# Head pairs of the stick-breaking group in a written-out order, and sums of weight halves by accumulating transfers

## What is computed

```python
def stick_breaking(q, k, v):             # 8 heads of 128
    ...
        z = jnp.einsum('bthd,bshd->bhts', qb, k).astype(jnp.float32) * d_h ** -0.5
        mask = key_pos[None, :] < t_pos[:, None]
        lo = jnp.where(mask, jax.nn.log_sigmoid(-z), 0.0)
        rc = lax.cumsum(lo, axis=3, reverse=True)
        log_a = jax.nn.log_sigmoid(z) + (rc - lo)
        a = jnp.where(mask, jnp.exp(log_a), 0.0)
        return jnp.einsum('bhts,bshd->bthd', a.astype(v.dtype), v)

def squared_relu_mlp(n, w_up, w_down):   # 1024 -> 4096 -> 1024, once in each layer
    return jnp.square(jax.nn.relu(n @ w_up)) @ w_down
```

## Time and profile before

| | us |
|---|---|
| median of 3 runs | 1587.18 |
| lowest, highest | 1586.47, 1589.25 |
| the profiled execution's own time | 1587.28 |
| its span in the trace | 1585.4 |
| TensorE busy | 1562.2 |
| VectorE, ScalarE, GpSimd busy | 1036.8, 726.8, 678.2 |

### The profile page before, as it was taken

How to read it: one execution, slowest core, us unless ns; L and a number is a source line. 1 busy time by engine, 2 the same in 40 slices (tenths; PEclk the granted TensorE clock), 3 DMA queues, 4 the chain that set the end, 5 groups by cost and what they waited for, 6 DMA issues and landing times.

```text
span 1585.4 us, 20551 instructions
## 1 busy us (share of the span) xinstructions
PE 1562.2 (99%) x7570; PEld 1283.4 (81%) x7570; DVE 1036.8 (65%) x1343; ACT 726.8 (46%) x1085; POOL 678.2 (43%) x666
## 2 busy tenths in 40 slices
PE   9999999999999999999999999989999999999999
PEld 7888787787778898888888888768886888888887
DVE  7424554675678977458584848867777557584847
ACT  6323433324245655434353435566775443444434
POOL 0002120104346443285666667422333474757574
PEclk9999999999999999999999999989999999999999
DMA  7232222232211221323223231222120414141321
GB/s 245 80 106 80 79 79 79 95 106 84 103 53 54 93 66 66 135 80 117 97 106 106 87 126 40 70 77 71 63 80 27 160 54 159 54 145 68 134 80 54
DMA packets 25731, 145.07 MB, mean 92 GB/s; under 512 B 3936, under 2 KB 5680, under 8 KB 9264
## 3 DMA queue, kind: packets, MB, share of 16 engines
q1 hardware_dynamic: 25648, 143.95, 26.4%
HBM read 141.84 MB, written 2.10 MB: 91 GB/s over the span
## 4 chain that ended last, share of the span: by engine, by line
PE 88%; DVE 9%; ACT 2%; issue 1%; POOL 0%; DVEq 0%; ACTq 0%; POOLq 0%
PE ps_G L613 20%; PE ps_G L615 20%; PE ps_G L614 20%; PE ps_C L1245 5%; PE ps_C L1244 5%; PE ps_C L1243 5%; PE ps_C L699 1%; PE ps_AV L1076 1%; PE ps_AV L1244 1%; PE ps_AV L1243 1%; PE ps_AV L1245 1%; DVE wide L2619 1%; DVE top L2615 1%; PE ps_C L713 1%; DVE wide L2809 1%
## 5 line engine op out<-in xcount | busy, mean ns | idle before, releaser
L613 PE MATMUL ps_G<-ch,wh 128*128 128x512 f32 x800 | 320.0, 400 | 0.7 <-DVE cl L2279 0.5
L615 PE MATMUL ps_G<-ch,wl 128*128 128x512 f32 x800 | 312.3, 390 | 0.0
L614 PE MATMUL ps_G<-cl,wh 128*128 128x512 f32 x800 | 312.2, 390 | 0.0
L2925 DVE TENSOR_TENSOR wl<-raw,wh 128x1024 fp32r<-128x1024 f32 (+1 forms) x104 | 180.7, 1756 | 30.5 <-ACT wh L1878 25.1
L613 PE MATMUL ps_G<-nh,wh 128*128 128x512 f32 x504 | 199.7, 396 | 0.4 <-DVE h L2487 0.2
L615 PE MATMUL ps_G<-nh,wl 128*128 128x512 f32 x504 | 196.3, 390 | 0.0
L614 PE MATMUL ps_G<-nl,wh 128*128 128x512 f32 x504 | 196.2, 389 | 0.0
L613 PEld LDWEIGHTS ps_G<-ch,wh 128*128 128x128 f32 x800 | 150.8, 188 | 39.9 <-issue 7.6
L614 PEld LDWEIGHTS ps_G<-cl,wh 128*128 128x128 f32 x800 | 150.7, 188 | 33.8 <-issue 3.4
L615 PEld LDWEIGHTS ps_G<-ch,wl 128*128 128x128 f32 x800 | 150.6, 188 | 31.7
L2214 DVE TENSOR_TENSOR wl<-raw,wh 128x2048 fp32r<-128x2048 f32 x46 | 108.6, 2360 | 62.1 <-ACT wh L1385 58.9
(11 more groups left out here) (429 smaller groups left out, 3185.6 us busy)
## 6 DMA issues: line engine op xcount, KB each, us to landing
raw<-wst SPq DMA_DIRECT2D x96, 1024.0 KB, 4.9
raw<-quart_d SPq DMA_DIRECT2D x16, 1024.0 KB, 4.9
tabs<-quart_d SPq DMA_DIRECT2D x8, 1024.0 KB, 7.1
mixed_buffers<-quart_d SPq DMA_DIRECT2D x8, 1024.0 KB, 5.3
raw<-wst SPq DMA_DIRECT2D x8, 256.0 KB, 6.9
out<-wide SPq DMA_DIRECT2D x8, 256.0 KB, 2.0
h<-xT SPq DMA_DIRECT2D x7, 256.0 KB, 6.9
raw<-wst SPq DMA_DIRECT2D x2, 512.0 KB, 5.9
```

What stands on the lines that cost most here:

```text
L613: mm(o, ah, bh, start=first, stop=False)
L614: mm(o, ah, bl, start=False, stop=False)
L615: return mm(o, al, bh, start=False, stop=last)
L2925: return tt(lo, x, hi.bitcast(F), ALU.subtract)
```

## The change

**Stick-breaking.** In group 0, the split of weight tile 1 moves up on both engines: on ScalarE ahead of the second `evac_qk`, on VectorE ahead of `diagonals_of` (a product with the identity, from which the row scales of the values come). The weights of head 12, the first of the group, are formed in group 0 instead of group 1: on ScalarE the softplus is the last step there, and the last root (`rsqrt(("qk", qk0 + 3))`) goes to group 1; on VectorE the first half stands ahead of `apply(3)` and the second inside it. In group 1 ScalarE does the first `evac_qk`, the root, the exponential and then the split (before: split, softplus, evacuation, exponential), and TensorE turns the scores ahead of the statistic of block 0. Groups 2 and 3 keep their order.

**Feed-forward.** The sums of weights are made by transfers that add to their destination (`accum_op=ALU.add`), issued on GpSimd's queue. They can't subtract, so the scheme is taken with the opposite sign of the right column: T3 = B22 + B12, T1 = B12 + B11, T2 = B11 + B12 + B22, T4 = B21 + T2. GpSimd's value sums and the second pair change sign to match, and the accumulators of the right column subtract. SyncE loads B22 a second time, into `t3` (`load_third`). T2 takes two transfers, from DRAM, the second of which waits for the first (`t2_part`); T4's source is on the chip. Each sum has a semaphore of its own, for the whole sum rather than for each half.

**End of the first feed-forward half.** VectorE's `low(4, 2)` stands ahead of `final_add(3)`.

```diff
+            def load_third(pt):
+                sp.dma_start(t3, quart_d[pt.f, pt.p, B22]).then_inc(t3_load, 16)
...
                 load_quarter(pt, B12, b12)
+                load_third(pt)
                 load_quarter(pt, B22, b22)
...
-                    sp.wait_ge(weight_sums, pt.sums_w + 8)
+                    sp.wait_ge(t4_in, 16 * (pt.g + 1))
                     sp.wait_ge(half_lo, pt.half(2, 1))
                     load(t % 2, t)
                     if not pt.last:
+                        sp.wait_ge(half_lo, pt.half(3, 1))
+                        load_third(Part(f, p + 1))
                         sp.wait_ge(half_lo, pt.half(4, 1))
                         load_quarter(Part(f, p + 1), B12, b12)
...
                 if name == "stick" and g == 1:
                     head_stat(("qk", qk0 - 1))
-                block_(1, 0, P)
-                head_stat(("qk", qk0))
-                if prev is not None:
+                    block_(1, 0, P)
+                    do_turns(0)
+                    head_stat(("qk", qk0))
+                else:
+                    block_(1, 0, P)
+                    head_stat(("qk", qk0))
                     do_turns(0)
...
                     evac_qk(0, 0)
+                    split(st, 1)
                     evac_qk(1, 1)
-                    split(st, 1)
...
+                    values_out(wide[:, 13, :], st, 5, 1)
                     rsqrt(("qk", qk0 + 2))
-                    values_out(wide[:, 13, :], st, 5, 1)
-                    rsqrt(("qk", qk0 + 3))
+                    weights(hd)
                     return
-                split(st, 0)
-                if prev is not None:
+                if g == 1:
+                    evac_qk(0, 0)
+                    rsqrt(("qk", qk0 - 1))
+                    exponential(prev)
+                    split(st, 0)
+                else:
+                    split(st, 0)
                     weights(prev)
-                evac_qk(0, 0)
-                if prev is not None:
+                    evac_qk(0, 0)
                     exponential(prev)
...
-                            act.wait_ge(weight_sums, pt.sums_w + W_SUMMED[i] + a + 1)
+                            act.wait_ge(W_SUMMED[i], 16 * (pt.g + 1))
...
-                    def weight_sum(dst, x, y):
...
+                    def add_weights(dst, x, sem_):
+
+                        g.dma_start(dst, quart_d[f, p, x] if isinstance(x, int) else x, accum_op=ALU.add).then_inc(sem_, 16)
...
+                    pool.wait_ge(t3_load, 16 * (pt.g + 1))
+                    add_weights(t3, B12, t3_in)
                     pool.wait_ge(quarter_in[B12], 16 * (pt.g + 1))
-                    pool.wait_ge(quarter_in[B22], 16 * (pt.g + 1))
+                    add_weights(b12, B11, t1_in)
                     if pt.g:
                         pool.wait_ge(half_lo, pt.halves)
-                    weight_sum(t3, b22, b12)
                     pair_sums(0)
                     pair_sums(1)
-                    pool.wait_ge(quarter_in[B11], 16 * (pt.g + 1))
-                    weight_sum(b12, b12, b11)
                     pair_sums(2)
                     pool.wait_ge(half_lo, pt.half(0, 1))
-                    pool.wait_ge(weight_sums, pt.sums_w + 4)
-                    weight_sum(b11, b22, b12)
+                    add_weights(b11, B12, t2_part)
+                    pool.wait_ge(t2_part, 16 * (pt.g + 1))
+                    add_weights(b11, B22, t2_in)
                     pair_sums(3)
                     pool.wait_ge(half_lo, pt.half(1, 1))
-                    pool.wait_ge(weight_sums, pt.sums_w + 6)
-                    weight_sum(b21, b21, b11)
+                    pool.wait_ge(t2_in, 16 * (pt.g + 1))
+                    add_weights(b21, b11, t4_in)
...
+                    split(st, 1)
                     diagonals_of(tmp[:, 5, :])
-                    split(st, 1)
                     apply(0, lambda: token_scales(2))
                     apply(1)
                     split(st, 2)
                     apply(2)
-                    apply(3)
+                    weights(hd, part=0)
+                    apply(3, lambda: weights(hd, part=1))
                     return
-                if prev is not None:
+                if prev is not None and (soft or g > 1):
                     weights(prev)
...
                 low(4, 1)
-                add_up(6, X, 0, 1)
+                add_up(6, X, 0, 1, ALU.subtract)
+                low(4, 2)
                 final_add(3)
-                low(4, 2)
```

More of the change, by code:

```diff
@@ L84, in __init__ @@
         self.first, self.last = p == 0, p == 3
-        self.halves, self.sums_w, self.sums_a = 14 * self.g, 8 * self.g, 16 * self.g
+        self.halves, self.sums_a = 14 * self.g, 16 * self.g
         self.adds = (4 * ADDS + 2) * f + ADDS * p
@@ L242, in build @@
         hid_set, quarter_in = sem("hid_set"), [sem(f"quarter_in{q}") for q in range(4)]
-        weight_sums, value_sums = sem("weight_sums"), sem("value_sums")
+        t1_in, t2_part, t2_in, t3_load, t3_in, t4_in = (sem(n) for n in (
+            "t1_in", "t2_part", "t2_in", "t3_load", "t3_in", "t4_in"))
+        value_sums = sem("value_sums")
         half_hi, half_lo, half_done = sem("half_hi"), sem("half_lo"), sem("half_done")
@@ L442, in build @@
         RING = (0, 1, 2, 3, 0, 2, 1)
-        W_SUMMED = {3: 0, 4: 2, 2: 4, 5: 6}
+        W_SUMMED = {2: t2_in, 3: t3_in, 4: t1_in, 5: t4_in}
         BACK = ("C2", "AV", "SX", "ST", "C2", "AV", "SX", "ST")
@@ L1895, in second_pair @@
                         act.wait_ge(value_sums, pt.sums_a + 4 * c + 3)
-                        A(ring_hi[:, 2:4, c, :], wide[:, 2 * c, :].rearrange("p (s n) -> p s n", s=2), ACT.Copy).then_inc(
+                        A(ring_hi[:, 2:4, c, :], wide[:, 2 * c, :].rearrange("p (s n) -> p s n", s=2), ACT.Copy, scale=-1.0).then_inc(
                             second_pair_hi, 1)
@@ L2113, in layer @@
                     b11, b21 = part_weights(pt)[0:2]
-                    def weight_sum(dst, x, y):
-                        for a in range(2):
-                            for n in range(4 * a, 4 * a + 4):
-                                w = slice(n * TW, (n + 1) * TW)
-                                ins = g.tensor_tensor(dst[:, w], x[:, w], y[:, w], ALU.subtract)
-                            ins.then_inc(weight_sums, 1)
+                    def add_weights(dst, x, sem_):
+                        g.dma_start(dst, quart_d[f, p, x] if isinstance(x, int) else x, accum_op=ALU.add).then_inc(sem_, 16)
                     def value_sum(n, dst, x, y, op):
@@ L2132, in pair_sums @@
                         pool.wait_ge(hid_set, 8 * pt.g + 2 * c + 2)
-                        value_sum(n, s1[:, c, :], a21, a22, ALU.add)
-                        value_sum(n + 1, a21, a11, a21, ALU.subtract)
+                        value_sum(n, s1[:, c, :], a22, a21, ALU.subtract)
+                        value_sum(n + 1, a21, a21, a11, ALU.subtract)
                         pool.wait_ge(first_pair_lo, 4 * pt.g + c + 1)
                         pool.wait_ge(value_sums, n + 2)
-                        value_sum(n + 2, a11, s1[:, c, :], a11, ALU.subtract)
+                        value_sum(n + 2, a11, a11, s1[:, c, :], ALU.add)
                         pool.wait_ge(value_sums, n + 3)
-                        value_sum(n + 3, a12, a12, a11, ALU.subtract)
+                        value_sum(n + 3, a12, a11, a12, ALU.subtract)
                     if pt.first and not f:
@@ L2781, in rotated, with weights @@
                     dve.wait_ge(q_rot, n + 1)
-                def weights(hh, whole=True, last=None):
+                def weights(hh, whole=True, last=None, part=None):
                     Sb = MIX_Sb[side(hh)]
@@ L2801, in weights @@
                     for n, banks in enumerate(HALVES):
+                        if part not in (None, n):
+                            continue
                         dve.wait_ge(sp_log, 2 * (hh - 12) + n + 1)
@@ L2935, in second_pair, with add_up @@
                         dve.wait_ge(second_pair_hi, 4 * pt.g + c + 1)
-                        subtract(ring_hi[:, 2:4, c, :], ring_lo[:, 2:4, c, :],
-                                 wide[:, 2 * c, :].rearrange("p (s n) -> p s n", s=2)).then_inc(second_pair_lo, 1)
-                    def add_up(i, banks, t, n):
+                        stt(out=ring_lo[:, 2:4, c, :], in0=wide[:, 2 * c, :].rearrange("p (s n) -> p s n", s=2),
+                            scalar=-1.0, in1=ring_hi[:, 2:4, c, :].bitcast(F), op0=ALU.mult,
+                            op1=ALU.subtract).then_inc(second_pair_lo, 1)
+                    def add_up(i, banks, t, n, op=ALU.add):
                         dve.wait_ge(half_done, pt.half(i, 1))
@@ L2944, in add_up @@
                             to = accumulator(2 * t + b, n)
-                            tt(to, to, ps[banks[b]][:], ALU.add).then_inc(acc_added, 1)
+                            tt(to, to, ps[banks[b]][:], op).then_inc(acc_added, 1)
```

(6 more changed lines are left out.)

## The result

The changed kernel took **1630.8 us** (median of 4 runs, 1628.3 to 1633.5) beside 1587.0 us for the kernel before (1586.5 to 1589.3): ratio 1.0276, 95% interval 1.026 to 1.0293. It is 44 us slower. The forecast was 1578.8 us, with a range of 1571 to 1612; the sign was wrong and the time lies outside the range.

The account below looks back on a forecast made before the run. TensorE, busy 99% of the span, was taken as the bound, leaving only idle time and slow clock to win. Span 1585.4 - 8 (opening) - 0.4 (low(4, 2)) = 1577.0, transfers 0, giving 1578.8 us measured; range 1571 to 1612.

Parts of the forecast that it names:

- the middle: Feed-forward weight sums: 6.1 us for each accumulating 1 MB transfer, so T2 is in at 804.7 and nothing is late.
- The upper end: Feed-forward weight sums: an accumulating megabyte also reads its destination, 7.4 us, making T2 2.1 us late in each part.
- the lower end: Feed-forward weight sums: an accumulating megabyte takes 4.9 us, as a plain load of the same array does; nothing late.
- The price of the clock behind a pause: Feed-forward, behind each pause before product 2: 1.2 us of slow clock, from 1.7 us behind the old 2.54 us pause.
- Rival A: Feed-forward: T2's chain of two transfers ends late, eight pauses; 1606 us at 7.4 us per transfer; chance 0.36.
- The opening: Start of stick-breaking: the new order gains 8 us, from 5 to 11.
- near tie: Opening, head pair 0: TensorE reaches the scores at 1039.5 with inputs ready at 1039.1; 2 to 3 us counted.
- Rival B: Opening of stick-breaking: new waits replace old ones, so 3 us gained instead of 8, 1584 us; chance 0.07.
- low(4, 2) ahead of an addition: End of the first feed-forward half: moving the correction ahead gains 0.4 us, from 0 to 0.5.
- GpSimd's sums removed for 0 us: Feed-forward: taking 257 us of weight sums off GpSimd is by itself worth nothing, as TensorE never waited for them.
- T1, T3, T4 and the signs: Feed-forward: T3 and T1 have over 40 us of cover, T4 is wanted after 16 us, moved signs cost 0 us.
- Rival C: Feed-forward: accumulating transfers delay the load of the next part's second tile, 1 us a part, 1587 us; chance 0.04.

Follow-up runs that it names:

- e1: Kernel before with only the new order of the head pairs and low(4, 2), weight sums still on GpSimd: 1579.7 us, ratio 0.9964.
- e9: Second run of the kernel before with the new order alone, weight sums on GpSimd: 1579.8 us, ratio 0.9951.
- e3: Changed kernel with T2 made by one accumulating transfer, B11 += T3: 1576.4 us, ratio 0.994 to the kernel before.
- e10: Second run of the changed kernel with T2 made by one transfer from T3: 1577.5 us, ratio 0.9935 to the kernel before.
- e8: Kernel before with old order, weight sums by four accumulating transfers, T2 by one from T3: 1584.8 us, ratio 0.9984.
- e4: Changed kernel with all five transfers of a part as plain copies, so weight sums are not computed: 1580.4 us, ratio 0.9965 to the kernel before.
- e6: Changed kernel with B12 added twice, so three transfers in a row for T2 (wrong by one B12): 1692.1 us in a single execution.
- e5: Changed kernel with both T2 transfers cut into halves with semaphores of their own: 1581.8 us, ratio 0.9969 to the kernel before.

## Why the prediction was wrong, step by step

**The price of an accumulating megabyte: the step that failed.** The prediction said "I take the middle, 6.1 us", with 4.9 and 7.4 as ends. Measured: 8.0, above both ends. The rest of that step held. GpSimd issued the first transfer at 797.3; VectorE's split of B11 ahead of it stands 4.6 us later than before (793.6 against 789.0), behind the pause of part 0, so in the times of the kernel before that is 792.7 (792.5 was said). And 6.35 us was all that a transfer could take. From the first issue to ScalarE's copy are 16.3 us; less 12.7, that is 3.6 us of pause; the row has 3.8. With the right duration the same working gives the right pause.

**The upper end was nearly right, the middle was not.** The upper end was 4.9 us for a plain load of SyncE and 2.5 us for as much data again, 7.4. Measured are 4.9, 0.3 for GpSimd's queue and 2.8 for the adding: 8.0. So the model of the upper end, that what goes with bytes costs double, holds: busy queues move 197 GB/s while they add and 424 while they load, and by these rates (an estimate) 1 MB takes 5.3 us in place of 2.5. It missed by 0.3 us on GpSimd's queue and by 0.3 on the bytes. The error that turned the sign was to take the middle between this model and the plain load: the lower end priced the adding at nothing, which no row supported, and the middle priced it at half.

The Trainium skill (Collectives: The Full Stack, The bandwidth ceiling: the fold count and why AG ≠ RS ≠ AR) has adding, in large transfers between cores, at about half the rate of a copy. The trace agrees on the rate (197 against 424 GB/s), and from issue to landing the ratio is 1.54, since part of the time does not go with bytes. The estimate by its ratio, 7.2 us, had the right sign for the kernel where mine had not, and I gave it no weight.

**The price of the clock behind a pause.** Rival A took 1.2 us for each of the eight pauses, from the one old pause of 2.54 us. Measured: 2.6. With the 3.6 us of pause rival A's own sum is 1578.8 + 8 x (3.6 + 1.2) = 1617 us; with 2.6 it is 1628, against 1630.8. So the mechanism of the loss was on record, with 0.36, and two of its terms were too small. Of the chance only 0.16 lay above 1612 us. (A and half of C make 0.38 for slower; the prediction has 0.37.)

**The opening.** Said: 8 us, with pauses of 4.6 us left and 2 of slow clock. Measured: 8.1 us by the landmarks, 7.9 in e1 and e9; pauses of 0.89, 0.77, 0.48, 0.66 and 1.75, 4.6 us together; slow clock 1.6. Part of that agreement is luck, as two details were off and cancelled: the "near tie" of the row scales of head pair 0 became a wait of 0.77 us, and the turned scores waited for ScalarE 0.5 us, not 1.9. Block 2 of group 1 was to start at 1059.2; in e1, with the old feed-forward half ahead of it, it starts at 1059.09. Rival B falls.

**low(4, 2) ahead of an addition.** Said: 0.4 us. Measured: nothing. The wait for `cl` there is 0.54 to 0.56 us in the changed kernel and in e1, e3, e9 and e10 with the new order, and 0.54 before and in e8 with the old one.

**GpSimd's sums removed for 0 us.** Measured with the chain out of the way: 2.0 to 3.3 us, of which 0.8 to 0.9 us in the first feed-forward half can be put down to it. VectorE's subtractions of 128 x 1024 fell from 1.51 to 1.35 us from `raw`, and from 1.46 and 1.49 to 1.22 from the other two tiles (1.25 was said), and two waits of TensorE, of 0.4 and 0.2 us, are gone; that the one comes of the other is likely, not shown. GpSimd is busy 445 us, not 430: its 40 DMA issues take 0.9 us each, 36 us together, where 430 left 9 for them.

**T1, T3, T4 and the signs.** Said: no cost. No wait of TensorE for them in the changed kernel or in e3, though T1 takes 15 us. Rival C (loads collide) falls too. GpSimd does stand 7.4 us in the wait for T2's first transfer with pair sums of chunk 3 behind it, and ScalarE waits 3.7 us for those; they end in time.

**What would show it.** The prediction named eight waits of `ps_C` with a clock under 1 behind, and ScalarE's idle time put down to a transfer into `raw`; both are there. It expected them put down to VectorE's `wl`; the profile puts them down to "issue". Whoever searches only for the named releaser misses the largest wait of the kernel.

**A version that beats both.** The new order with T2 made from T3 by one transfer takes 1576.4 and, a second time, 1577.5 us, 0.6% under the kernel before. The order alone, with the sums on GpSimd, takes 1579.7.

## What to carry to other kernels

An operation that no row of the trace shows must be priced with a wide upper end, and where its result is wanted within a margin of a few per cent, one run that times it alone is worth more than any middle between bounds. Count transfers in a row, not bytes: a chain whose second link reads what the first wrote pays the full time from issue to landing twice, and a sum that lies in SBUF already, or halves with semaphores of their own, take the chain away. Price a pause of TensorE of 4 to 12 us, the lengths measured here, at its own length plus 2 to 2.6 us of slow clock on average, and let single ones lie between 1.4 and 3.1.

## What the runs showed of the hardware

- An accumulating transfer of 1 MB from DRAM into SBUF takes 8.0 us, the same transfer without adding 5.2; from SBUF to SBUF 6.9 to 7.0 and 4.5. Busy queues move 197 GB/s while they add and 424 while they load. Half a megabyte takes 5.9 us, in this kernel beside one other transfer of its kind.
- GpSimd is busy 0.9 us for each accumulating DMA of 1 MB that it issues (the changed kernel), and 0.55 us for the same without adding (e4).
- The slow clock behind a pause of 12 us costs TensorE no more (2.1 us on average, e6, one execution) than behind one of 4 us (2.6 us, the changed kernel).
- The same pauses of 0.5, 0.65 and 1.75 us in a row were followed by a slow stretch of about 1.6 us in the order alone (e1, e9), in e4, in e5 and in the changed kernel, and by none in e3, e10 and e6. The cause is open; in e1 and e10 the pauses stand at the same times to 0.1 us.
